# Attention values in two passes: V's high and low parts of one head as one stationary operand

## The chip, the cores and the metric

The kernel runs on one core of a Trainium2 chip. The metric is the device time of one execution in microseconds. TensorE (PE) multiplies matrices into PSUM, VectorE (DVE) and ScalarE (ACT) do the elementwise work, GpSimd (POOL) a little of it, and the DMA queues are driven from SyncE (SP) and GpSimd.

## The reference, cut to what matters

One layer of a mixer (stick-breaking attention, pooling, cross-attention into 256 memory rows, three sigmoid gates), then a mixture of 16 experts with two experts per token. All in float32, 512 tokens, model width 1024, 8 heads of 64 and 4 cross heads of 64. The change touches the last line of each attention:

```python
# stick-breaking attention, per head and block of 128 queries
z = jnp.einsum('bhqd,bhkd->bhqk', qi, k) * scale
log_1m = jnp.where(strict, jax.nn.log_sigmoid(-z), 0.0)
tail = lax.cumsum(log_1m, axis=3, reverse=True) - log_1m
a = jnp.where(strict, jnp.exp(jax.nn.log_sigmoid(z) + tail), 0.0)
return jnp.einsum('bhqk,bhkd->bhqd', a, v)

# cross-attention into memory, per head
p = jax.nn.softmax(s, axis=-1)
o = jnp.einsum('bhqm,bmhd->bqhd', p, v)
```

## The kernel before

Matrix products run on operands of type float32r. To keep float32's precision each operand is split into a high part (a copy, which rounds) and a low part (the difference to the original), and a product is three passes: high x high, high x low, low x high. The helper `three` (lines 464 to 468) issues them. ScalarE makes high parts, VectorE low parts. Weights come in chunks of 128 x 2048 through a ring of three slots (`split_hi`, `split_lo`); a chunk is a stage's unit, and TensorE frees it by `chunk_used`. There is no scheduler: each engine's order is the order of the code, and semaphores tie them.

Stages around the change, by TensorE: projections and cross-attention (`cross_scores`, `cross_transpose`, `cross_out`, rounds r = 0 and 1 of two heads each), then the loop over heads n = 0 to 8 (lines 1269 to 1293). In round n TensorE issues `tails(n)` (20 passes), a projection (24 passes of 512 columns, or 48 of 256) in rounds 0 to 4, 6 and 8 only, then `values(n - 1)` (lines 1233 to 1248) and `scores(n + 2)`. So rounds 5 and 7 have no projection. ScalarE computes the logarithm of head n + 1 (three passes over 128 x 1280, `logarithm`), the exp that gives `attn`, the high parts; VectorE computes `softplus` and the low parts. `attn_hi` exists once, `attn` and `attn_lo` twice.

`values(m)` computes one head's output, transposed, into bank 7 of PSUM: for each of 4 blocks of keys, 512, 384, 256 and 128 query columns wide, the stationary operand is 128 columns of V, which are two heads (64 columns each), and only the 64 rows of the head in question are read out (line 916 for the high part, 1762 for the low). The next `values` waits until both have read the bank (`av_l`, line 1238). `cross_out(r)` does the same with V of the memory: 2 heads x 2 blocks x 3 passes of 512 columns, read out at lines 842 to 847 and 1693 to 1698. `v_hi_part` and `v_lo_part` (lines 820, 1676) make V's two parts, a quarter at a time.

After the heads come four rounds of gates and branches (`rest`), the output product, routing, and the experts.

Of the kernel before, what the change touches and what calls it, by code (L numbers as in the profile page):

```python
# [28 lines left out]
P = 128  # L29
# [66 lines left out]
def build_trunk(nc, x, mem, norm_mix, norm_mem, w_in, w_pool, pool_scale, w_kv_mem, w_up_sb,  # L96
# [80 lines left out]
    v_hi = sb("v_hi", [P, TB, SBW], F32R, "m", 32 * KB)  # L177
    v_lo = sb("v_lo", [P, TB, SBW], F32R, "m", 40 * KB)
# [25 lines left out]
    vm_hi = sb("vm_hi", [P, MB, XW], F32R, "t", 12 * KB)  # L204
    vm_lo = sb("vm_lo", [P, MB, XW], F32R, "t", 14 * KB)
# [74 lines left out]
    with ctx:  # L280
# [52 lines left out]
        xo_ps = sem("xo_ps")  # L333
        xo_h = sem("xo_h")
# [10 lines left out]
        av_ps = sem("av_ps")  # L345
        av_h = sem("av_h")
# [410 lines left out]
        def _(act):  # L757
# [51 lines left out]
            proj_hi(C_VM, vm_hi[:, :, :], bank(1))  # L809
# [32 lines left out]
            def cross_o(r):  # L842
# [18 lines left out]
            qk_hi(2, 2)  # L861
            cross_o(0)
            split_hi(act, K(C_PAIR[2]))
# [28 lines left out]
            cross_o(1)  # L892
            soften(0)
            split_hi(act, K(C_V[1]))
            qk_hi(4, 6)
            for n in range(HEADS + 1):
# [15 lines left out]
                if n >= 1:  # L912
                    m = n - 1
                    rows = slice(DH * (m % 2), DH * (m % 2) + DH)
                    act.wait_ge(av_ps, m + 1)
                    act.activation(sbT_hi[rows, m // 2, :], bank(7)[rows, :], ACT.Copy).then_inc(av_h, 1)
                if n == 3:
                    split_hi(act, K(C_MERGE))
                if n == 5:
                    split_hi(act, K(C_MERGE + 1))  # L920

# [137 lines left out]
        def _(pe):  # L1059
# [86 lines left out]
            def cross_out(r):  # L1146
# [42 lines left out]
            pe.wait_ge(xo_l, 1)  # L1189
# [43 lines left out]
            def values(m):  # L1233
# [3 lines left out]
                if m >= 1:  # L1237
                    pe.wait_ge(av_l, m)
# [28 lines left out]
            pe.wait_ge(xo_l, 2)  # L1267
# [285 lines left out]
        def _(dve):  # L1553
# [99 lines left out]
            dve.wait_ge(proj_h, 3)  # L1653
            less(flat(vm_lo[:, :, :]), bank(1), flat(vm_hi[:, :, :])).then_inc(proj_l, 1)
# [436 lines left out]
```

## Time and profile before

| | us |
|---|---|
| median of 3 runs | 769.59 (769.48 to 770.74) |
| the profiled execution | 769.72 |
| its span, first to last instruction | 767.9 |
| TensorE busy | 713.7 (93%) |
| VectorE busy | 507.8 (66%) |
| ScalarE busy | 407.8 (53%) |
| mean granted clock of TensorE | 0.972 of full speed |

The profile is one execution, taken by the hardware profiler. Times of rows are from the start of the span. TensorE's matmul rows overlap (a row's duration holds the pipeline's fill and drain), so what a pass costs in a stream is the distance between two starts, not its duration. A bracket at the end of a row gives the engine's idle time before it and what released it. The granted clock is 1.00 at 2.4 GHz and 0.50 at 1.2 GHz. Helpers' rows carry the helper's line: L466 to L468 are the three passes of `three`, L443 and L449 are the ring's high and low parts, L1612 is `less`, VectorE's subtraction.

### The profile page before, as it was taken

How to read it: one execution, taken by the hardware profiler on the slowest of the kernel's cores; microseconds unless marked ns; L12 is line 12 of the kernel's file. 1: busy time of each engine (PE TensorE's matmuls, PEld its weight loads, DVE VectorE, ACT ScalarE, POOL GpSimd, SP SyncE). 2: the span in 40 equal slices, each digit the busy share in tenths (PEclk: the TensorE clock that was granted, in tenths of full speed). 3: DMA queues.
4: the chain of work that ended last, by engine and by line, in shares of the span. 5: the costliest groups of instructions: out<-in, count | busy, mean ns of one | idle time of the engine just before them, and what ended most of it. 6: DMA issues, size and time to landing. Idle time of an engine off the chain costs nothing.

```text
span 767.9 us, 9989 instructions
## 1 busy us (share of the span) xinstructions
PE 713.7 (93%) x3587; PEld 598.3 (78%) x3587; DVE 507.8 (66%) x548; ACT 407.8 (53%) x413; POOL 109.5 (14%) x112
## 2 busy tenths in 40 slices
PE   4999998899999999999999999999999999999920
PEld 3898887789888888888888957888888888888810
DVE  5768563456632507062444588999999999999928
ACT  6726555456632214032232427787878787887712
POOL 5000000000000000000000121333334344331120
PEclk9999998999999999999999999999999999999975
DMA  8552321000023322322377169999999999999444
GB/s 275 172 165 55 110 72 38 1 1 28 15 93 113 101 78 90 115 96 96 128 258 299 39 254 362 395 392 373 372 371 371 365 381 364 371 377 374 184 166 189
DMA packets 85169, 155.47 MB, mean 202 GB/s; under 512 B 6229, under 2 KB 37071, under 8 KB 84628
## 3 DMA queue, kind: packets, MB, share of 16 engines
q1 hardware_dynamic: 78452, 137.39, 50.4%
q0 software_dynamic: 6688, 17.69, 6.0%
q8 instruction: 19, 0.31, 0.2%
q14 instruction: 10, 0.08, 0.0%
HBM read 150.64 MB, written 12.58 MB: 213 GB/s over the span
## 4 chain that ended last, share of the span: by engine, by line
PE 88%; DVE 5%; ACT 2%; issue 2%; DMA 2%; POOL 1%; POOLq 0%; DVEq 0%; ACTq 0%
PE ps L466 27%; PE ps L468 26%; PE ps L467 26%; PE ps L1447 2%; PE ps L1227 1%; PE ps L1504 1%; PE ps L1373 1%; PE ps L1473 1%; PE ps L1229 1%; PE ps L1401 1%; DMA y_rows<-ye,y_col 1%; PE ps L1073 1%; DMA y_in<-y_rows 1%; DVE x L2060 1%; DVE x L2067 1%
## 5 line engine op out<-in xcount | busy, mean ns | idle before, releaser
L449 DVE TENSOR_TENSOR ring_lo<-raw_a,ring_hi 128x2048 fp32r<-128x2048 f32 (+2 forms) x58 | 115.5, 1994 | 97.2 <-ACT ring_hi L443 97.2
L449 DVE TENSOR_TENSOR ring_lo<-raw,ring_hi 128x2048 fp32r<-128x2048 f32 x71 | 161.3, 2289 | 12.4 <-ACT ring_hi L443 10.9
L443 ACT ACTIVATE ring_hi<-raw 128x2048 fp32r<-128x2048 f32 x71 | 136.3, 1920 | 19.8 <-PE ps L468 19.8
L466 PE MATMUL ps<-hT_hi,ring_hi 128*128 128x512 f32 x288 | 113.9, 396 | 4.4 <-DVE v_lo L1612 2.2
L443 ACT ACTIVATE ring_hi<-raw_a 128x2048 fp32r<-128x2048 f32 (+2 forms) x58 | 97.4, 1680 | 32.3 <-PE ps L468 32.2
L468 PE MATMUL ps<-hT_hi,ring_lo 128*128 128x512 f32 x288 | 112.8, 392 | 0.0
L467 PE MATMUL ps<-hT_lo,ring_hi 128*128 128x512 f32 x288 | 112.7, 391 | 0.0
L466 PE MATMUL ps<-ring_hi,xT_hi 128*128 128x512 f32 x240 | 94.8, 395 | 1.8 <-DVE xT_lo L1918 1.8
L468 PE MATMUL ps<-ring_hi,xT_lo 128*128 128x512 f32 x240 | 93.8, 391 | 0.0
L467 PE MATMUL ps<-ring_lo,xT_hi 128*128 128x512 f32 x240 | 93.6, 390 | 0.0
L466 PEld LDWEIGHTS ps<-hT_hi,ring_hi 128*128 128x128 f32 x288 | 54.4, 189 | 16.7 <-DVE v_lo L1612 2.4
L468 PEld LDWEIGHTS ps<-hT_hi,ring_lo 128*128 128x128 f32 x288 | 54.5, 189 | 11.6
L467 PEld LDWEIGHTS ps<-hT_lo,ring_hi 128*128 128x128 f32 x288 | 54.5, 189 | 10.9
L723 POOL DMA_INDIRECT y_rows<-ye,y_col x16 | 33.0, 2060 | 177.9 <-DVE ye L2003 174.9
L466 PEld LDWEIGHTS ps<-ring_hi,xT_hi 128*128 128x128 f32 x240 | 45.1, 188 | 11.1 <-DVE xT_lo L1918 2.1
L468 PEld LDWEIGHTS ps<-ring_hi,xT_lo 128*128 128x128 f32 x240 | 45.0, 188 | 9.4
L467 PEld LDWEIGHTS ps<-ring_lo,xT_hi 128*128 128x128 f32 x240 | 45.1, 188 | 9.1
L466 PE MATMUL ps<-ring_hi,aT_hi 128*128 128x512 f32 x120 | 48.1, 401 | 0.0
L468 PE MATMUL ps<-ring_hi,aT_lo 128*128 128x512 f32 x120 | 47.0, 392 | 0.0
L467 PE MATMUL ps<-ring_lo,aT_hi 128*128 128x512 f32 x120 | 46.9, 391 | 0.0
L933 ACT ACTIVATE sig<-ps 128x1024 f32<-128x1024 f32 x8 | 8.2, 1029 | 69.0 <-PE ps L468 69.0
L708 POOL DMA_INDIRECT xe<-h_rows,x_col x15 | 35.0, 2332 | 12.9 <-POOL x_col L705 12.9
(339 smaller groups left out, 1269.2 us busy)
## 6 DMA issues: line engine op xcount, KB each, us to landing
raw<-in_w_down SPq DMA_DIRECT2D x25, 1024.0 KB
raw<-in_w_gate SPq DMA_DIRECT2D x47, 512.0 KB
raw<-in_w_up SPq DMA_DIRECT2D x47, 512.0 KB
raw_a<-in_w_in SPq DMA_DIRECT2D x15, 1024.0 KB
raw_a<-in_w_gate SPq DMA_DIRECT2D x17, 512.0 KB
raw_a<-in_w_up SPq DMA_DIRECT2D x17, 512.0 KB
raw_a<-in_w_down SPq DMA_DIRECT2D x7, 1024.0 KB
raw_a<-in_w_in SPq DMA_DIRECT2D x10, 512.0 KB, 7.9
```

The costliest lines, as they stand in the source:

```text
L443: act.activation(ring_hi[:, c[0] % SPLIT, 0:width], buf[:, 0:width], ACT.Copy).then_inc(hi_ready, 1)
L449: dve.tensor_tensor(ring_lo[:, s, 0:width], buf[:, 0:width], ring_hi[:, s, 0:width].bitcast(F32), ALU.subtract).then_inc(lo_ready, 1)
L466: pe.matmul(out_ap, l_hi, r_hi, start=start, stop=False, skip_group_check=True)
L467: pe.matmul(out_ap, l_hi, r_lo, start=False, stop=False, skip_group_check=True)
L468: return pe.matmul(out_ap, l_lo, r_hi, start=False, stop=stop, skip_group_check=True)
L708: pool.indirect_dma_start(xe[b][:, :], None, h2_rows[:, :], bass.IndirectOffsetOnAxis(x_col[b][:, :].bitcast(U32), 0), bounds_check=S - 1, ...
L723: pool.indirect_dma_start(y_rows[:, :], bass.IndirectOffsetOnAxis(y_col[b][:, :].bitcast(U32), 0), ye[b][:, :], None, bounds_check=2 * S - ...
L933: act.activation(sig[:, i, :, :], gate_pair(i), ACT.Sigmoid).then_inc(g_sig, 1)
L1073: ins = pe.transpose(bank(k)[:, t * P:(t + 1) * P], xn[:, t, k * P:(k + 1) * P], ident[:, :])
L1227: pe.matmul(zz[:, o:o + w], lhs[:, :], soft_hi[:, j:j + w], start=False, stop=False, skip_group_check=True)
L1229: ins = pe.matmul(zz[:, o:o + w], lhs[:, :], soft_lo[:, j:j + w], start=False, stop=jb == TB - 1, skip_group_check=True)
L1447: ins = pe.transpose(bank(2, 2)[:, k * P:(k + 1) * P], xe[b][:, k * P:(k + 1) * P], ident[:, :])
```

## The change

V's two parts go into one array of four blocks of 64 columns per pair of heads, in the order high(even), low(even), low(odd), high(odd). The stationary operand of a head is then its own two blocks side by side, 128 columns again (`stacked`). One pass with the high part of the attention weights and one with the low part give, in PSUM, the high part of V against both in the head's own 64 rows, and the low part of V against both in the other 64 rows. The two halves have to be added: ScalarE copies the other half into the head's rows of an SBUF array (`value_x`, `cross_x`), VectorE adds the PSUM half to it (`value_sum`, `cross_sum`), and the high and low parts are then taken from the SBUF sum (`value_hi`, `value_lo`, `cross_o`), for the values one round later. TensorE waits for the sum (`av_sum`, `xo_sum`) instead of the low part. The product low x low, which three passes leave out, is included. V's parts are written by two instructions of 256 columns instead of one of 512.

```diff
-    v_hi = sb("v_hi", [P, TB, SBW], F32R, "m", 32 * KB)
-    v_lo = sb("v_lo", [P, TB, SBW], F32R, "m", 40 * KB)
+    v_st = sb("v_st", [P, TB, SBW // P, 4, DH], F32R, "m", 32 * KB)
+    sbT_f = sb("sbT_f", [P, 4, S], F32, "m", 72 * KB)
+    xaT_f = sb("xaT_f", [P, 2, S], F32, "m", 92 * KB)
...
+        def stacked(st, h):
+            return st[:, 2 * h:2 * h + 2, :].rearrange("p b d -> p (b d)")
+        def blocks(ap):
+            return ap.rearrange("p (r h d) -> p r h d", h=2, d=DH)
...
@@ ScalarE @@
-                act.activation(v_hi[:, 2 * (i % 2):2 * (i % 2) + 2, 256 * (i // 2):256 * (i // 2) + 256],
-                               bank(b).rearrange("p (t n) -> p t n", t=2), ACT.Copy).then_inc(v_h, 1)
+                for u in range(2):
+                    ins = act.activation(v_st[:, 2 * (i % 2) + u, 2 * (i // 2):2 * (i // 2) + 2, 0:4:3, :],
+                                         blocks(bank(b)[:, u * 256:u * 256 + 256]), ACT.Copy)
+                ins.then_inc(v_h, 1)
...
+            def cross_x(r):
                 act.wait_ge(xo_ps, r + 1)
                 for h in range(2):
-                    rows = slice(DH * h, DH * h + DH)
-                    ins = act.activation(xaT_hi[rows, r, :], bank(6 * r + h)[rows, :], ACT.Copy)
-                ins.then_inc(xo_h, 1)
+                    ins = act.activation(xaT_f[head_rows(h), r, :], bank(6 * r + h)[head_rows(1 - h), :], ACT.Copy)
+                ins.then_inc(xo_x, 1)
+            def value_x(m):
+                act.wait_ge(av_ps, m + 1)
+                act.activation(sbT_f[head_rows(m % 2), m // 2, :], bank(7)[head_rows(1 - m % 2), :],
+                               ACT.Copy).then_inc(av_x, 1)
+            def value_hi(m):
+                rows = head_rows(m % 2)
+                act.wait_ge(av_sum, m + 1)
+                act.activation(sbT_hi[rows, m // 2, :], sbT_f[rows, m // 2, :], ACT.Copy).then_inc(av_h, 1)
...
                 if n >= 1:
-                    m = n - 1
-                    rows = slice(DH * (m % 2), DH * (m % 2) + DH)
-                    act.wait_ge(av_ps, m + 1)
-                    act.activation(sbT_hi[rows, m // 2, :], bank(7)[rows, :], ACT.Copy).then_inc(av_h, 1)
+                    value_x(n - 1)
+                if n >= 2:
+                    value_hi(n - 2)
...
@@ TensorE @@
                     for m in range(MB):
-                        ins = three(pe, bank(6 * r + h), vm_hi[:, m, r * P:(r + 1) * P], vm_lo[:, m, r * P:(r + 1) * P],
-                                    pT_hi[:, 2 * h + m, :], pT_lo[:, 2 * h + m, :], m == 0, m == MB - 1)
+                        pe.matmul(bank(6 * r + h), stacked(vm_st[:, m, r, :, :], h), pT_hi[:, 2 * h + m, :],
+                                  start=m == 0, stop=False, skip_group_check=True)
+                        ins = pe.matmul(bank(6 * r + h), stacked(vm_st[:, m, r, :, :], h), pT_lo[:, 2 * h + m, :],
+                                        start=False, stop=m == MB - 1, skip_group_check=True)
...
                 if m >= 1:
-                    pe.wait_ge(av_l, m)
+                    pe.wait_ge(av_sum, m)
...
-                    ins = three(pe, bank(7)[:, sbk * P:], v_hi[:, sbk, pr * P:(pr + 1) * P],
-                                v_lo[:, sbk, pr * P:(pr + 1) * P], attn_hi[:, o:o + w], attn_lo[m % 2][:, o:o + w],
-                                sbk == 0, sbk == TB - 1)
+                    pe.matmul(bank(7)[:, sbk * P:], stacked(v_st[:, sbk, pr, :, :], m % 2), attn_hi[:, o:o + w],
+                              start=sbk == 0, stop=False, skip_group_check=True)
+                    ins = pe.matmul(bank(7)[:, sbk * P:], stacked(v_st[:, sbk, pr, :, :], m % 2),
+                                    attn_lo[m % 2][:, o:o + w], start=False, stop=sbk == TB - 1, skip_group_check=True)
...
-            pe.wait_ge(xo_l, 2)
+            pe.wait_ge(xo_sum, 2)
             project_qk(4, 6)
...
@@ VectorE @@
+            def value_sum(m):
+                rows = head_rows(m % 2)
+                dve.wait_ge(av_x, m + 1)
+                dve.tensor_tensor(sbT_f[rows, m // 2, :], bank(7)[rows, :], sbT_f[rows, m // 2, :], ALU.add).then_inc(av_sum, 1)
...
+                if n >= 1:
+                    value_sum(n - 1)
                 if n < HEADS:
                     dve.wait_ge(a_exp, n + 1)
-                    if n >= 1:
-                        dve.wait_ge(av_ps, n)
                     dve.tensor_copy(attn_hi[:, :], attn[n % 2][:, :]).then_inc(a_h, 1)
...
-                if n >= 1:
-                    m = n - 1
-                    rows = slice(DH * (m % 2), DH * (m % 2) + DH)
-                    dve.wait_ge(av_h, m + 1)
-                    less(sbT_lo[rows, m // 2, :], bank(7)[rows, :], sbT_hi[rows, m // 2, :]).then_inc(av_l, 1)
+                if n >= 2:
+                    value_lo(n - 2)
```

How the instructions then stand. First TensorE, values of head 1, before (the first passes; the words are output, moving operand, stationary operand, shape and semaphores waited for):

```order
L466 MATMUL ps<-attn_hi,v_hi 128x512 [waits av_l,a_l]
L467 MATMUL ps<-attn_lo_148,v_hi 128x512
L468 MATMUL ps<-attn_hi,v_lo 128x512
L466 MATMUL ps<-attn_hi,v_hi 128x384
L467 MATMUL ps<-attn_lo_148,v_hi 128x384
L468 MATMUL ps<-attn_hi,v_lo 128x384
L466 MATMUL ps<-attn_hi,v_hi 128x256
```

and after, from the same place:

```order
L1282 MATMUL ps<-attn_hi,v_st 128x512 [waits av_sum,a_l]
L1284 MATMUL ps<-attn_lo_148,v_st 128x512
L1282 MATMUL ps<-attn_hi,v_st 128x384
L1284 MATMUL ps<-attn_lo_148,v_st 128x384
L1282 MATMUL ps<-attn_hi,v_st 128x256
L1284 MATMUL ps<-attn_lo_148,v_st 128x256
```

The four passes with V's low part are gone, and the first pass waits for the sum.

VectorE in rounds 5 and 6 of the loop over heads, before. `attn_hi` and `attn_lo` belong to heads 5 and 6, `soft` and `soft_lo` to heads 6 and 7, `sbT_lo` to heads 4 and 5, and `ring_lo` is the low part of a weight chunk:

```order
L1724 SCALAR_TENSOR_TENSOR soft<-ps,log_in 128x1280 [waits tail_ps,z_ln]
L1729 TENSOR_TENSOR soft_lo<-soft,soft_hi 128x1280 [waits soft_h]
L1752 CAST attn_hi<-attn_146 128x1280 [waits av_ps,a_exp]
L1754 TENSOR_TENSOR attn_lo_148<-attn_146,attn_hi 128x1280 [waits a_h]
L1612 TENSOR_TENSOR sbT_lo<-ps,sbT_hi 64x512 [waits av_h]
L449 TENSOR_TENSOR ring_lo<-raw_a,ring_hi 128x2048 [waits hi_ready]
L1724 SCALAR_TENSOR_TENSOR soft<-ps,log_in 128x1280 [waits tail_ps,z_ln]
L1729 TENSOR_TENSOR soft_lo<-soft,soft_hi 128x1280 [waits soft_h]
L1752 CAST attn_hi<-attn_145 128x1280 [waits av_ps,a_exp]
L1754 TENSOR_TENSOR attn_lo_147<-attn_145,attn_hi 128x1280 [waits a_h]
L1612 TENSOR_TENSOR sbT_lo<-ps,sbT_hi 64x512 [waits av_h]
```

and after, where `sbT_f` is the sum of heads 4 and 5, and `sbT_lo` belongs to head 3:

```order
L1780 SCALAR_TENSOR_TENSOR soft<-ps,log_in 128x1280 [waits tail_ps,z_ln]
L1785 TENSOR_TENSOR soft_lo<-soft,soft_hi 128x1280 [waits soft_h]
L1753 TENSOR_TENSOR sbT_f<-ps,sbT_f 64x512 [waits av_x]
L1809 CAST attn_hi<-attn_146 128x1280 [waits a_exp]
L1811 TENSOR_TENSOR attn_lo_148<-attn_146,attn_hi 128x1280 [waits a_h]
L1650 TENSOR_TENSOR sbT_lo<-sbT_f,sbT_hi 64x512 [waits av_h]
L454 TENSOR_TENSOR ring_lo<-raw_a,ring_hi 128x2048 [waits hi_ready]
L1780 SCALAR_TENSOR_TENSOR soft<-ps,log_in 128x1280 [waits tail_ps,z_ln]
L1785 TENSOR_TENSOR soft_lo<-soft,soft_hi 128x1280 [waits soft_h]
L1753 TENSOR_TENSOR sbT_f<-ps,sbT_f 64x512 [waits av_x]
L1809 CAST attn_hi<-attn_145 128x1280 [waits a_exp]
L1811 TENSOR_TENSOR attn_lo_147<-attn_145,attn_hi 128x1280 [waits a_h]
```

The sum stands ahead of `attn_hi` and waits for ScalarE's copy; the low part stands where it stood, for the head before. Between `soft_lo` and the next `soft` there is one instruction of 64 x 512 more.

ScalarE in round 5, before (`log_in` is the logarithm of head 7):

```order
L888 ACTIVATE soft_hi<-soft 128x1280 [waits z_soft]
L916 ACTIVATE sbT_hi<-ps 64x512 [waits av_ps]
L443 ACTIVATE ring_hi<-raw_a 128x2048 [waits chunk_used,raw_full2]
L880 ACTIVATE log_in<-ps 128x1280 [waits z_soft,z_ps]
L882 ACTIVATE log_in<-log_in 128x1280 [waits act_c]
L884 ACTIVATE log_in<-log_in 128x1280 [waits act_c]
```

and after:

```order
L922 ACTIVATE soft_hi<-soft 128x1280 [waits z_soft]
L870 ACTIVATE sbT_f<-ps 64x512 [waits av_ps]
L876 ACTIVATE sbT_hi<-sbT_f 64x512 [waits av_sum]
L448 ACTIVATE ring_hi<-raw_a 128x2048 [waits chunk_used,raw_full2]
L914 ACTIVATE log_in<-ps 128x1280 [waits z_soft,z_ps]
L916 ACTIVATE log_in<-log_in 128x1280 [waits act_c]
L918 ACTIVATE log_in<-log_in 128x1280 [waits act_c]
```

A second copy of 64 x 512 stands ahead of the chunk's high part and of the next logarithm.

## Rows read from the trace of the kernel before

**Rows 1.** The page's 40 slices: TensorE busy, its granted clock, DMA engines, in tenths.
```profile
PE   4999998899999999999999999999999999999920
...
PEclk9999998999999999999999999999999999999975
DMA  8552321000023322322377169999999999999444
```

**Rows 2.** The page's chain of work that ended last, shares by engine.
```profile
PE 88%; DVE 5%; ACT 2%; issue 2%; DMA 2%; POOL 1%; POOLq 0%; DVEq 0%; ACTq 0%
```

**Rows 3.** Waits of TensorE, 112 to 222 us: us in total, times, longest.
```profile
PE ps L1209 <- ACT attn L905: 3.2, 2, 2.9
PE ps L466 <- DVE v_lo L1612: 2.2, 1, 2.2
PE ps L1227 <- DVE soft_lo L1729: 0.6, 1, 0.6
PE ps L466 <- DVE sbT_lo L1612: 0.6, 1, 0.6
```

**Rows 4.** Stretches with a low clock: us, PE busy (instructions), granted clock, DMA, GB/s.
```profile
120.00:128.00 8.00, 7.91 (x36) 0.57 0.00 0
137.00:142.00 5.00, 5.00 (x17) 0.66 0.02 3
428.00:432.00 4.00, 4.00 (x15) 0.57 0.01 4
```

**Rows 5.** Timeline of TensorE, values of one head: start us, us, instruction; then what follows.
```profile
169.05 0.39 PE L466 MATMUL ps<-attn_hi,v_hi 128*128 128x512 f32 x1
...
170.91 0.40 PE L1209 MATMUL ps<-negmask,identb 128*128 128x128 bf16 x4
```

**Rows 6.** Timeline of TensorE, first eight passes of the tails of head 0, and the next.
```profile
114.29 0.39 PE L1227 MATMUL ps<-soft_hi,negtri 128*128 128x512 f32 x1
...
115.52 0.39 PE L1227 MATMUL ps<-soft_hi,negtri 128*128 128x384 f32 x1
```

**Rows 7.** Timeline of TensorE, cross output of round 1 (12 passes), and what follows.
```profile
103.07 0.40 PE L466 MATMUL ps<-pT_hi,vm_hi 128*128 128x512 f32 x1
...
105.82 0.40 PE L1209 MATMUL ps<-negmask,identb 128*128 128x128 bf16 x4
```

**Rows 8.** Timeline of VectorE, attn_lo of an ordinary head.
```profile
159.39 1.49 DVE L1754 TENSOR_TENSOR attn_lo<-attn,attn_hi 128x1280 fp32r<-128x1280 f32 x1
```

**Rows 9.** Timeline of ScalarE, late heads.
```profile
193.00 0.57 ACT L916 ACTIVATE sbT_hi<-ps 64x512 fp32r<-64x512 f32 x1
...
195.28 1.22 ACT L880 ACTIVATE log_in<-ps 128x1280 f32<-128x1280 f32 x1
```

**Rows 10.** Timeline of VectorE, late heads.
```profile
199.61 1.47 DVE L1724 SCALAR_TENSOR_TENSOR soft<-ps,log_in 128x1280 f32<-128x1280 f32 x1
202.42 1.50 DVE L1729 TENSOR_TENSOR soft_lo<-soft,soft_hi 128x1280 fp32r<-128x1280 f32 x1 [1.34 <-ACT soft_hi L888]
205.16 0.83 DVE L1752 CAST attn_hi<-attn 128x1280 fp32r<-128x1280 f32 x1 [1.25 <-PE ps L468]
206.03 1.49 DVE L1754 TENSOR_TENSOR attn_lo<-attn,attn_hi 128x1280 fp32r<-128x1280 f32 x1
207.55 0.69 DVE L1612 TENSOR_TENSOR sbT_lo<-ps,sbT_hi 64x512 fp32r<-64x512 f32 x1
```

**Rows 11.** Timeline of TensorE, late heads (a bracket: idle us before it, releaser).
```profile
191.54 0.38 PE L1209 MATMUL ps<-negmask,identb 128*128 128x128 bf16 x4 [0.33 <-ACT attn L905]
...
204.90 0.45 PE L1227 MATMUL ps<-soft_hi,negtri 128*128 128x512 f32 x1
...
208.39 0.47 PE L466 MATMUL ps<-attn_hi,v_hi 128*128 128x512 f32 x1 [0.55 <-DVE sbT_lo L1612]
```

**Rows 12.** Timeline of VectorE, eight instructions of 256 columns.
```profile
31.71 3.22 DVE L1623 SCALAR_TENSOR_TENSOR memT_lo<-ps,gains,memT_hi 128x256 fp32r<-128x256 f32 x8
```

**Rows 13.** The page's groups: TensorE's loads of stationary operands.
```profile
L466 PEld LDWEIGHTS ps<-hT_hi,ring_hi 128*128 128x128 f32 x288 | 54.4, 189 | 16.7 <-DVE v_lo L1612 2.4
```

More of the change, by code:

```diff
@@ L203, in build_trunk @@
     km_lo = sb("km_lo", [P, 2, MEM], F32R, "t", 10 * KB)
-    vm_hi = sb("vm_hi", [P, MB, XW], F32R, "t", 12 * KB)
-    vm_lo = sb("vm_lo", [P, MB, XW], F32R, "t", 14 * KB)
+    vm_st = sb("vm_st", [P, MB, XW // P, 4, DH], F32R, "t", 12 * KB)
     U0 = 16
@@ L333, in build_trunk @@
         xo_ps = sem("xo_ps")
+        xo_x = sem("xo_x")
+        xo_sum = sem("xo_sum")
         xo_h = sem("xo_h")
@@ L345, in build_trunk @@
         av_ps = sem("av_ps")
+        av_x = sem("av_x")
+        av_sum = sem("av_sum")
         av_h = sem("av_h")
@@ L462, in width_of, with head_rows @@
             return CW
+        def head_rows(h):
+            return slice(DH * h, DH * h + DH)
+        def stacked(st, h):
+            return st[:, 2 * h:2 * h + 2, :].rearrange("p b d -> p (b d)")
+        def blocks(ap):
+            return ap.rearrange("p (r h d) -> p r h d", h=2, d=DH)
         def three(pe, out_ap, l_hi, l_lo, r_hi, r_lo, start, stop):
@@ L808, in _ @@
             proj_hi(C_KM, km_hi[:, :, :], bank(0))
-            proj_hi(C_VM, vm_hi[:, :, :], bank(1))
+            after(act, K(C_VM))
+            for m in range(MB):
+                act.activation(vm_st[:, m, :, 0:4:3, :], blocks(bank(1)[:, m * XW:(m + 1) * XW]),
+                               ACT.Copy).then_inc(proj_h, 1)
             def qk_hi(n, b):
@@ L861, in _ @@
             qk_hi(2, 2)
+            cross_x(0)
+            split_hi(act, K(C_PAIR[2]))
             cross_o(0)
-            split_hi(act, K(C_PAIR[2]))
             act.wait_ge(pool_d, 2)
@@ L891, in _ @@
             v_hi_part(1, 3)
-            cross_o(1)
+            cross_x(1)
             soften(0)
             split_hi(act, K(C_V[1]))
+            cross_o(1)
             qk_hi(4, 6)
@@ L920, in _ @@
                     split_hi(act, K(C_MERGE + 1))
+            value_hi(HEADS - 1)
             act.preload_act_table_set("sigmoid_and_others")
@@ L1188, in _ @@
             project_qk(3, 3)
-            pe.wait_ge(xo_l, 1)
+            pe.wait_ge(xo_sum, 1)
             project_v(0, 0)
@@ L1651, in _ @@
             link(dve.tensor_copy(pool_a[hi_r, 1, U0:], pool_b[hi_r, 1, U0:]))
-            dve.wait_ge(proj_h, 3)
-            less(flat(vm_lo[:, :, :]), bank(1), flat(vm_hi[:, :, :])).then_inc(proj_l, 1)
+            dve.wait_ge(proj_h, 2 + MB)
+            for m in range(MB):
+                ins = less(vm_st[:, m, :, 1:3, :], blocks(bank(1)[:, m * XW:(m + 1) * XW]), vm_st[:, m, :, 0:4:3, :])
+            ins.then_inc(proj_l, 1)
             def cross_max(r):
@@ L1677, in v_lo_part @@
                 dve.wait_ge(v_h, i + 1)
-                part = (slice(2 * (i % 2), 2 * (i % 2) + 2), slice(256 * (i // 2), 256 * (i // 2) + 256))
-                less(v_lo[:, part[0], part[1]], bank(b).rearrange("p (t n) -> p t n", t=2),
-                     v_hi[:, part[0], part[1]]).then_inc(v_l, 1)
+                for u in range(2):
+                    part = v_st[:, 2 * (i % 2) + u, 2 * (i // 2):2 * (i // 2) + 2, :, :]
+                    ins = less(part[:, :, 1:3, :], blocks(bank(b)[:, u * 256:u * 256 + 256]), part[:, :, 0:4:3, :])
+                ins.then_inc(v_l, 1)
             def cross_norm(r):
@@ L1691, in cross_t, with cross_sum, value_lo @@
                 less(flat(pT_lo[:, :, :]), bank(4, 4), flat(pT_hi[:, :, :])).then_inc(xt_l, 1)
+            def cross_sum(r):
+                dve.wait_ge(xo_x, r + 1)
+                for h in range(2):
+                    ins = dve.tensor_tensor(xaT_f[head_rows(h), r, :], bank(6 * r + h)[head_rows(h), :],
+                                            xaT_f[head_rows(h), r, :], ALU.add)
+                ins.then_inc(xo_sum, 1)
             def cross_o(r):
                 dve.wait_ge(xo_h, r + 1)
-                for h in range(2):
-                    rows = slice(DH * h, DH * h + DH)
-                    ins = less(xaT_lo[rows, r, :], bank(6 * r + h)[rows, :], xaT_hi[rows, r, :])
-                ins.then_inc(xo_l, 1)
+                less(xaT_lo[:, r, :], xaT_f[:, r, :], xaT_hi[:, r, :]).then_inc(xo_l, 1)
+            def value_lo(m):
+                rows = head_rows(m % 2)
+                dve.wait_ge(av_h, m + 1)
+                less(sbT_lo[rows, m // 2, :], sbT_f[rows, m // 2, :], sbT_hi[rows, m // 2, :]).then_inc(av_l, 1)
+            def value_sum(m):
+                rows = head_rows(m % 2)
+                dve.wait_ge(av_x, m + 1)
+                dve.tensor_tensor(sbT_f[rows, m // 2, :], bank(7)[rows, :], sbT_f[rows, m // 2, :], ALU.add).then_inc(av_sum, 1)
             cross_norm(0)
@@ L1710, in _ @@
             qk_lo(2, 2)
+            cross_sum(0)
+            cross_max(1)
             cross_o(0)
-            cross_max(1)
             split_lo(dve, K(C_PAIR[2]))
@@ L1732, in _ @@
             v_lo_part(1, 3)
-            cross_o(1)
+            cross_sum(1)
             soft_low(0)
             split_lo(dve, K(C_V[1]))
+            cross_o(1)
             qk_lo(4, 6)
@@ L1766, in _ @@
                     split_lo(dve, K(C_MERGE + 1))
+            value_lo(HEADS - 1)
             with dve.Fori(0, KD // 2) as dp:
```

4 lines of the change are left out of this document (3 added, 1 removed).

## The prediction

> **What bounds the kernel now.** I read the slices of the page first: TensorE is busy nine tenths or more of nearly every slice, at full clock except in a few places [rows 1]. The chain that ended last says the same: 88% of the span is TensorE, 5% VectorE, 2% ScalarE [rows 2]. So an instruction taken off TensorE is worth its issue interval, unless TensorE waits for something a little later anyway. The DMA engines are nine tenths busy in the expert stage [rows 1], but TensorE waits there only once, for VectorE, and the expert weights are requested as buffers come free, so a stage that starts earlier also loads earlier; I take an earlier start to pass through to the end unchanged.
>
> The change lies between 30 and 220 us. I therefore asked for TensorE's waits from 112 to 222 us, where the heads run: 3.2 us for ScalarE's exp (two times, the longest 2.9), 2.2 for the low part of V, 0.6 for soft_lo, 0.6 for sbT_lo [rows 3]. Everything else in that stretch is bound by TensorE. After the two longest waits the granted clock is at its lower level: 0.57 over the 8 us from 120 and 0.66 over the 5 us from 137, which is (1-0.57)x2x8 = 6.9 us and (1-0.66)x2x5 = 3.4 us at 1.2 GHz, in which half the time is lost. It is low again around 428 us, with no wait ahead of it [rows 4].
>
> **What goes.** Values of one head: twelve passes run from 169.05 to 170.91, 1.86 us [rows 5]. The change leaves eight, of the same four widths (512, 384, 256, 128 columns). What eight such passes take, two with each width, is shown by the first row of blocks of the tails: 114.29 to 115.52, 1.23 us [rows 6]. The saving is 1.86 - 1.23 = 0.63 us for each of eight heads, 5.0 us. Cross output: twelve passes of 512 columns from 103.07 to 105.82, 2.75 us [rows 7]; four of the twelve go, 0.92 us in each of two rounds, 1.8 us. Together 6.9 us if nothing else ends later. No pass becomes dearer: all stationary operands were and are 128 columns wide.
>
> The Trainium skill, page "TensorE: Matmul & The Clock Gate", section "Back-to-back issue gap", gives the isolated interval as columns/2.4 + 2.5 ns; by it the 40 passes would be worth 8 x 0.54 + 8 x 0.216 = 6.1 us (an estimate). The same section gives some 131 ns for a 512-column pass in a sustained stream, which would leave about 1 us of the 1.8 for the cross output. The trace has 2.75/12 = 0.229 us there [rows 7], near the first and far from the second, and the trace decides.
>
> **What is added, and what it lies beside.** Per head there is one more ScalarE instruction and one more VectorE instruction on 64 x 512. The old copies of that size take 0.57 us on ScalarE (0.6 where they don't follow another at once) and 0.69 on VectorE [rows 9, 10]. A ScalarE copy from one half of the partitions into the other is not in the trace. I take the old copy's 0.6 us, since neither its size nor its source changes; the bounds are 0.57 below and 1.2 above (crossing costs double). At 1.2 the cross output would reach project_qk(4) 1.2 us later and values(6) would start 0.6 later: 1.8 us of the gain lost.
>
> Heads 0 to 3. TensorE's next values block no longer waits for hi and lo, but only for copy plus sum, 0.6 + 0.69 = 1.3 us behind the block; it needs them a whole head later. But the sum now stands on VectorE ahead of the two attn instructions, which are what the next block really needs. Today attn_lo of an ordinary head ends at 159.39 + 1.49 = 160.9 for a block that starts at 169.05 [rows 5, 8]: 8.2 us of slack, against 0.6 + 0.69 = 1.3 us of delay. The low part (0.69) and ScalarE's hi copy (0.57) fall into idle time behind. All 4 x 0.63 = 2.5 us come through.
>
> Heads 4 to 7, where there is less other TensorE work between blocks. (1) scores(7) starts at 191.54 after a wait of 0.33 us for the exp of head 5 [rows 11]; this exp hangs on scores(6), not on values(4), which lies between. So values(4) becomes shorter and the wait longer, from 0.3 to 0.95 us: 0 of 0.63. (2) tails(6) waits for soft_lo, again behind scores(6): unchanged. (3) On ScalarE, value_x(4) and value_hi(3) now both stand ahead of the split of a weight chunk; the logarithm that began at 195.28 begins 0.5 to 0.6 us later [rows 9]. On VectorE value_sum(4) and value_lo(3), 1.38 us together, replace one sbT_lo of 0.69, so the chunk's low part ends up to 0.7 later, and softplus(7), which started at 199.61 right behind it, starts about 0.6 later. soft_lo(7) would then end at 202.42 + 1.50 + 0.6 = 204.5 [rows 10]. tails(7) started at 204.90 and could now start at 204.3, but gets its operand at 204.55: gain 0.3 instead of 0.6. (4) values(6) started at 208.39, behind sbT_lo (207.55 + 0.69 = 208.24) [rows 10, 11]. Now values(5) ends about 204.4, copy to 205.05, sum to 205.75, the two attn instructions (0.83 and 1.49) to 208.05: values(6) starts near 208.2, gain 0.2. (5) values(6) and values(7) then give 2 x 0.63 = 1.26, since a gate projection of 24 passes (24 x 0.229 = 5.5 us) lies ahead of values(7) and covers the 1.3 + 2.3 us of its operand. Sum for heads 4 to 7: 1.45 us.
>
> Cross output. Today two ScalarE copies and two VectorE subtractions follow it, and TensorE waits for the last; now two copies and two additions of the same size. The wait of project_qk(4) is a chain of the same length from the same point, so 1.8 us come through. The hi and lo splits behind it, now one 128 x 512 each, are off TensorE's path.
>
> V's split. Each part is now two instructions of 128 x 256 instead of one of 128 x 512. Eight VectorE instructions of 256 columns take 3.22 us, 0.40 each [rows 12], so 0.8 against 0.69: 0.1 longer. This counts once, in the wait of 2.2 us before project_qk(5), where v_lo is the last link: 0.1 us lost. Before scores(1) V's part 1 would end level with TensorE's arrival, but a delay there is swallowed by the wait for the cross output behind it.
>
> Sum: 2.5 + 1.45 + 1.8 - 0.1 = 5.7 us. Past the heads ScalarE starts its table load and the third gate chunk about 0.6 us later against TensorE, while TensorE has two gate projections (22 us) before it uses it: nothing. The profiled execution took 769.7 us (767.9 us of span and 1.8 around it), 0.1 above the median of the three runs, so 769.7 - 5.7 = **764.0 us**.
>
> **Rivals.**
> *The clock falls at a new place* (12%). TensorE's idle time between 190 and 209 us grows from 1.5 us in three pieces (0.33, 0.64, 0.55) to some 2.5 in four (0.95, 0.64, 0.3, 0.65). For it: at 428 us the clock is low with no wait at all [rows 4]. Against: pieces of 0.3 to 0.6 cost nothing today, and only waits of 2.2 us or more are followed by the low level in the heads. One such stretch of 3.4 us costs 1.7: 765.7; two 767.4. The reverse is as possible: one of today's stretches may be 3.4 us shorter or absent because work shifted under it, 762.3.
> *The saved passes turn into waits in all heads* (6%). If the ScalarE/VectorE chain bounded the ordinary heads too, only cross output and heads 6 and 7 would count, 1.8 + 1.3: 766.6. For it: heads 4 and 5 do so. Against: no wait at all from 148 to 190 us.
> *Slower* (4%). The sum ahead of attn_hi: value_x + value_sum put 1.3 us between the end of one block and attn_hi, and if TensorE waited for attn_lo at each of seven heads, that would be 7 x 1.3 = 9.0 against 5.7 saved: 769.7 + 3.3 = 773.0. It decides only where attn_lo ends later than 1.3 us before the block; the rows give 8.2 us in an ordinary head, and only head 6 is close; even 1.9 us a head, with the copy at its upper bound, fits into 8.2.
> *No change* (4%): the two-pass form does not go faster, because the stationary operand is loaded anew for each pass (each load 0.19 us [rows 13]) and paces the narrow ones. Against: the tails load anew each time as well [rows 6], 1.23/8 = 0.154 us a pass. It would give 769 to 770.
>
> **Numbers.** The likeliest case, 764.0, has 74%; its own range by the clock's stretches and the copy's bounds is 762.3 to 765.7. The whole range is 762.0 to 767.2. What a measurement of this kernel can tell from no change is 0.2%, 1.5 us. Faster 0.91, same 0.05, slower 0.04.
>
> **What would show it.** Values blocks of eight passes in 1.23 us and cross blocks in 1.83; the wait of scores(7) for attn at about 0.95 us; a new wait of tails(7) for soft_lo of some 0.3; values(6) waiting for attn_lo instead of sbT_lo; the wait for V's low part at 2.3; VectorE's additions at 0.69 and ScalarE's crossing copies at 0.6; the merge stage starting 5.7 us earlier, and the same distance at the end of the experts. It is wrong if crossing copies take over 1.2 us, if TensorE waits in heads 1 to 3, or if the expert stage waits for weights.

## The result and the profile after

The changed kernel takes **765.4 us** (median of 5 runs, 764.06 to 766.66); the kernel before, run on the same chip beside it, 769.75 us (769.48 to 770.74). The ratio is 0.9946, 95% interval 0.9931 to 0.996: 0.5% faster, 4.35 us. The forecast was 764.0 with a range of 762.0 to 767.2, so the time lies inside, 1.4 us above the point. The profiled execution took 765.4 us, its span 763.7, which is 4.2 less than the profiled span before.

The page's busy times and slices (TensorE, granted clock, DMA engines, in tenths):

```profile
PE 707.8 (93%) x3547; PEld 593.1 (78%) x3547; DVE 514.7 (67%) x563; ACT 414.8 (54%) x428; POOL 109.6 (14%) x112
...
PE   4999997999999999999999999999999999999920
...
PEclk9999998999899999999999999999999999999975
DMA  8562320000033231323476269999999999999444
```

TensorE has 40 instructions fewer (3587 before), VectorE and ScalarE have 15 more each. Beside [rows 1], the clock's row has one low slice more: slice 7 (115 to 134 us) is the low place after the long wait for exp, as before, and slice 11 (191 to 210 us) is new. Single slices of TensorE and of the DMA differ by a tenth or so. The chain that ended last is TensorE for 88% of the span, as in [rows 2].

The passes themselves. TensorE's timeline of round 1 of the cross output, with the instruction that follows (start us, us, instruction):

```profile
102.31 0.40 PE L1187 MATMUL ps<-pT_hi,vm_st 128*128 128x512 f32 x1
...
104.16 0.40 PE L1246 MATMUL ps<-negmask,identb 128*128 128x128 bf16 x4
```

and of the values of an ordinary head:

```profile
164.48 0.39 PE L1282 MATMUL ps<-attn_hi,v_st 128*128 128x512 f32 x1
...
165.70 0.40 PE L1246 MATMUL ps<-negmask,identb 128*128 128x128 bf16 x4
```

The distance of the starts counts, not the durations, which overlap. Eight cross passes take 104.16 - 102.31 = 1.85 us (twelve took 2.75 [rows 7]), eight passes of values 165.70 - 164.48 = 1.22 us (twelve: 1.86 [rows 5]).

TensorE's waits from 105 to 218 us (us in total, times, longest):

```profile
PE ps L1246 <- ACT attn L940: 3.9, 2, 2.9
PE ps L481 <- DVE v_st L1650: 2.3, 1, 2.3
PE ps L1282 <- DVE attn_lo L1811: 1.0, 1, 1.0
PE ps L1264 <- DVE soft_lo L1785: 0.6, 1, 0.6
PE ps L481 <- DVE xaT_f L1737: 0.4, 1, 0.4
```

Beside [rows 3], 0.7 us more for exp, and a wait of 1.0 for attn_lo where one of 0.6 for sbT_lo stood (the last row lies ahead of the window of [rows 3]). Where these are, TensorE's timeline tells (in brackets the idle us before the instruction and what ended them):

```profile
107.03 0.50 PE L481 MATMUL ps<-hT_hi,ring_hi 128*128 128x512 f32 x1 [0.37 <-DVE xaT_f L1737]
...
134.88 0.50 PE L481 MATMUL ps<-hT_hi,ring_hi 128*128 128x512 f32 x1 [2.31 <-DVE v_st L1650]
...
140.45 0.39 PE L1282 MATMUL ps<-attn_hi,v_st 128*128 128x512 f32 x1
...
185.69 0.38 PE L1246 MATMUL ps<-negmask,identb 128*128 128x128 bf16 x4 [0.96 <-ACT attn L940]
...
201.25 0.45 PE L1264 MATMUL ps<-soft_hi,negtri 128*128 128x512 f32 x1
...
205.20 0.50 PE L1282 MATMUL ps<-attn_hi,v_st 128*128 128x512 f32 x1 [1.02 <-DVE attn_lo L1811]
...
212.07 0.39 PE L1282 MATMUL ps<-attn_hi,v_st 128*128 128x512 f32 x1
```

The instructions of the kernel before that answer to these and are not in [rows 11], by its timeline:

```profile
108.69 0.50 PE L466 MATMUL ps<-hT_hi,ring_hi 128*128 128x512 f32 x1 [0.36 <-DVE xaT_lo L1612]
...
136.52 0.50 PE L466 MATMUL ps<-hT_hi,ring_hi 128*128 128x512 f32 x1 [2.25 <-DVE v_lo L1612]
...
143.73 0.39 PE L466 MATMUL ps<-attn_hi,v_hi 128*128 128x512 f32 x1
...
215.84 0.39 PE L466 MATMUL ps<-attn_hi,v_hi 128*128 128x512 f32 x1
```

How far ahead of before the changed kernel is, place by place:

| place | ahead, us | step |
|---|---|---|
| project_qk(4) | 1.66 | cross output |
| project_qk(5) | 1.64 | V's split, 0.02 lost |
| values(0) | 3.28 | no pass saved here: 1.64 from the clock |
| scores(7) | 5.85 | values(0) to (3) 2.57; values(4) nothing |
| values(6) | 3.19 | 2.66 given back |
| values(7) | 3.77 | values(6) 0.58 |
| first pass behind values(7) | 4.41 (217.69 before, 213.28 after) | values(7) 0.64 |
| end of the span | 4.2 | 0.2 given back |

The two jumps that belong to no pass are the clock's. Windows of TensorE (us, busy and instructions, granted clock, DMA share, GB/s):

```profile
120.00:128.00 8.00, 8.00 (x42) 0.58 0.00 0
137.00:142.00 5.00, 5.00 (x29) 1.00 0.01 3
188.00:196.00 8.00, 7.36 (x29) 0.57 0.01 3
424.00:428.00 4.00, 4.00 (x14) 0.61 0.01 4
```

The stretch of 0.66 from 137 to 142 us of [rows 4] is absent, which gives the 1.7 us of its 5 x 0.34. From 188 to 196, where the kernel before had full clock, it is 0.57: 7.36 busy us at that clock lose about 0.43 of themselves, 3.2 us. So the profiled 4.2 is no clean measure of the change, and a second one is needed.

**A measure without the clock.** Each run lists its span and its mean granted clock. TensorE sets the pace for most of the span, so I take (1 - clock) x span for the time lost at the lower level and compare kernels by span x clock. It is a measure for differences only: of the 21 us so counted in the kernel before, 14 stand in the last 28 us, where TensorE has no instruction and the profile lists a clock of 0.50 (740 to 768 us; in the changed kernel 736 to 764, also 0.50), and these 14 are the same in every kernel. The clock is given to 0.001 or so, 0.8 us in one run, so I use means over runs; +- is one standard error of the mean.

Before, 29 runs: clock 0.9710, product 746.1 (+-0.1). After, 5 runs: 0.9696 and 740.5 (+-0.2). The difference is **5.5 us** (+-0.2) for a sum of 5.7 forecast; about 1 us of it is then lost because the mean clock was 0.0014 lower. The 29 are the runs of before that stand beside the first four experiments, since those beside the changed kernel have no clock on record; 11 more on another chip, beside the last four experiments, give 746.1 too.

Runs with the same listed clock can be compared directly: at 0.970, 768.86 before (13 runs) and 763.60 after (2 runs), 5.3 us; at 0.972, 767.72 (10) and 762.3 (1), 5.4; at 0.968, 771.0 (1) and 764.65 (2), 6.4, with one run of before only. The clock is also what spreads runs of one kernel: those before at 0.974 lie at 766.25 us of span (2 runs).

### The profile page after: what moved, and what is told of

Its sections match the earlier page's. It is cut to its first block, busy times and chain, and to the rows that moved or that the text cites. A ratio compares the mean times of both kernels' runs of the same rounds, so it can differ in the third digit from the quotient of the medians.

```text
span 763.7 us, 9932 instructions
## 1 busy us (share of the span) xinstructions
PE 707.8 (93%) x3547; PEld 593.1 (78%) x3547; DVE 514.7 (67%) x563; ACT 414.8 (54%) x428; POOL 109.6 (14%) x112
## 4 chain that ended last, share of the span: by engine, by line
PE 88%; DVE 6%; issue 2%; ACT 2%; DMA 2%; POOL 1%; POOLq 0%; DVEq 0%; ACTq 0%
PE ps L481 26%; PE ps L482 25%; PE ps L483 25%; PE ps L1485 2%; PE ps L1264 1%; PE ps L1266 1%; PE ps L1542 1%; PE ps L1411 1%; PE ps L1511 1%; DMA y_rows<-ye,y_col 1%; PE ps L1439 1%; DMA y_in<-y_rows 1%; DVE x L2115 1%; DVE x L2122 1%; PE ps L1284 1%
```

## The experiments

### Cross output alone

The kernel before, with the two-pass form for the cross output only (with its copies and additions, which the cut leaves out); the values keep their three passes.

```diff
-                        ins = three(pe, bank(6 * r + h), vm_hi[:, m, r * P:(r + 1) * P], vm_lo[:, m, r * P:(r + 1) * P],
-                                    pT_hi[:, 2 * h + m, :], pT_lo[:, 2 * h + m, :], m == 0, m == MB - 1)
+                        pe.matmul(bank(6 * r + h), stacked(vm_st[:, m, r, :, :], h), pT_hi[:, 2 * h + m, :], ...)
+                        ins = pe.matmul(bank(6 * r + h), stacked(vm_st[:, m, r, :, :], h), pT_lo[:, 2 * h + m, :], ...)
```

> The kernel before with the cross output alone in two passes (values as before). Theory A (savings add up by pass count where nothing waits): the cross blocks take 1.83 us instead of 2.75, all later waits keep their lengths (2.91 before scores(2), 2.25 before project_qk(5), 0.33, 0.64, 0.55 in the late heads), and the time is 1.8 us below before at an equal share of the low clock. Rival B (the clock decides more than the passes): the time lies anywhere from 1.8 below to 1.8 above before, with the mean granted clock of each run explaining the rest; span x (1 - clock), taken off the span, should then still differ by 1.8 from before.

Measured: 768.63 us (12 runs, 765.98 to 770.59) beside 770.42 of before; ratio 0.9978 (0.9966 to 0.999). Span x clock 744.1, 2.0 below before. TensorE's waits are those of before to 0.1 us. Yet the clock is low from 192 to 196 us, after waits no longer than those in the kernel before. TensorE's timeline at the two waits, and its windows:

```profile
189.14 0.33 PE L1231 MATMUL ps<-negmask,identb 128*128 128x128 bf16 x3 [0.33 <-ACT attn L925]
...
192.28 0.76 PE L1249 MATMUL ps<-soft_hi,negtri 128*128 128x512 f32 x1 [0.63 <-DVE soft_lo L1758]
```

```profile
188.00:192.00 4.00, 3.32 (x23) 1.00 0.00 0
192.00:196.00 4.00, 3.73 (x15) 0.57 0.00 0
```

Nothing near these instructions was changed but their place in time, 2.4 us earlier than in the kernel before.

### Values alone

The changed kernel with the cross output back to three passes. Seen from the kernel before, this is the two-pass form for the values only (its copies and additions are again left out of the cut):

```diff
-                    ins = three(pe, bank(7)[:, sbk * P:], v_hi[:, sbk, pr * P:(pr + 1) * P],
-                                v_lo[:, sbk, pr * P:(pr + 1) * P], attn_hi[:, o:o + w], attn_lo[m % 2][:, o:o + w],
-                                sbk == 0, sbk == TB - 1)
+                    pe.matmul(bank(7)[:, sbk * P:], stacked(v_st[:, sbk, pr, :, :], m % 2), attn_hi[:, o:o + w], ...)
+                    ins = pe.matmul(bank(7)[:, sbk * P:], stacked(v_st[:, sbk, pr, :, :], m % 2), attn_lo[m % 2][:, o:o + w], ...)
```

> The changed kernel with the cross output back to three passes. Theory A: values blocks of 1.23 us; heads 0 to 3 give 2.5 us, head 4 nothing (wait before scores(7) 0.95), heads 6 and 7 give 1.3, V's split costs 0.1: some 3.8 us below before at an equal share of the low clock, and 1.8 above the changed kernel. Rival B: no sum of the two parts is visible because the low-clock stretches move by themselves; then the difference to before is within 1.8 of 3.8 either way, run by run, following the mean granted clock.

Measured: 767.66 us (12 runs, 765.55 to 770.73), ratio 0.997 (0.9957 to 0.9984). Span x clock 742.2 (+-0.2), 3.9 below before; the forecast's steps for values and V's split give 2.5 + 1.45 - 0.1 = 3.85. With the 2.0 (+-0.2) of the cross output this makes 5.9 (+-0.3) for 5.5 (+-0.2) in the whole: the parts add up within their errors. Two of its waits of TensorE are the ones that the changed kernel has more than before:

```profile
PE ps L1237 <- ACT attn L933: 3.9, 2, 2.9
...
PE ps L1273 <- DVE attn_lo L1793: 1.0, 1, 1.0
```

### The short waits filled with passes

The changed kernel, with seven passes of 512 columns around scores(7), whose output nobody reads.

```diff
+                if n == 5:
+                    pe.wait_ge(v_l, 4)
+                    for _ in range(4):
+                        pe.matmul(bank(6), hT_hi[:, 0, 0:P], hT_hi[:, 0, :], start=True, stop=True, skip_group_check=True)
                 if n + 2 < HEADS:
                     scores(n + 2)
+                if n == 5:
+                    for _ in range(3):
+                        pe.matmul(bank(6), hT_hi[:, 0, 0:P], hT_hi[:, 0, :], start=True, stop=True, skip_group_check=True)
```

> The changed kernel with seven more 512-column passes whose result nobody reads: four after values(4), in the wait before scores(7), three after scores(7), in the wait before tails(6). The work is not needed; it keeps TensorE busy. Theory C (the longer wait of 0.96 us with the 0.64 us behind it brings the low clock at 189 us): the stretch of half clock from 189 to 195 us disappears and the time falls by 1.7 to 3.4 us against the changed kernel. Rival D (where the clock falls has nothing to do with this wait): the stretch is still there in some executions and the time is the changed kernel's within 0.3 us, the passes being hidden in the waits.

Measured: 764.34 us (6 runs, 764.02 to 766.87), ratio 0.9935 (0.9919 to 0.9952). Work added on TensorE costs nothing that can be measured, since it stands where TensorE waited (the wait before scores(7) is gone): span x clock 740.7 (+-0.3), the changed kernel's 740.5. In its profile's windows of TensorE the clock from 185 to 200 us is full, but low from 136 to 140, inside the stretch where the changed kernel's was full:

```profile
136.00:140.00 4.00, 4.00 (x12) 0.60 0.00 0
185.00:200.00 15.00, 15.00 (x84) 1.00 0.07 19
```

The mean clock over its runs is 0.9703 beside 0.9696. That is too little to tell apart with so few runs, and its median lies inside the changed kernel's range. So theory C has its stretch gone but not its gain of 1.7 to 3.4 us. One profile each can't tell whether the passes moved the stretch or whether it would have moved by itself.

### The kernel before, with head 4 short

The kernel before, whose head 4 leaves out the product with V's low part (four passes).

```diff
+                    if m == 4:
+                        pe.matmul(bank(7)[:, sbk * P:], v_hi[:, sbk, pr * P:(pr + 1) * P], attn_hi[:, o:o + w], ...)
+                        ins = pe.matmul(bank(7)[:, sbk * P:], v_hi[:, sbk, pr * P:(pr + 1) * P], attn_lo[m % 2][:, o:o + w], ...)
+                        continue
```

> The kernel before with head 4 computed without its four passes of V's low part (this part of the product is left out for head 4). Nothing else changes. The chain from scores(6) through the exp is untouched, so the wait before scores(7) grows from 0.33 to 0.95 us and no time is saved at full clock. Theory C: a stretch of half clock appears behind 190 us and the time rises by 1.7 to 3.4 us above before. Rival D: no such stretch; the time is that of before within 0.3 us.

Measured: median of ten executions 769.64 us (two more, of 1474 and 2552 us, are left out of it), ratio 0.999 (0.9977 to 1.0002), span x clock 746.3 (+-0.1) beside 746.1. Four passes went and the time stayed; they became a wait, as the forecast's step (1) has it. But the clock did not fall behind this longer wait, by TensorE's timeline and window:

```profile
191.56 0.33 PE L1209 MATMUL ps<-negmask,identb 128*128 128x128 bf16 x3 [0.96 <-ACT attn L905]
...
194.70 0.50 PE L1227 MATMUL ps<-soft_hi,negtri 128*128 128x512 f32 x1 [0.64 <-DVE soft_lo L1735]
```

```profile
185.00:200.00 15.00, 13.40 (x85) 1.00 0.00 0
```

After reading the changed profile, my theory was that the wait of 0.33 us, grown to 0.96, brings the low stretch at 188 us. As a rule it falls here: 0.96 and 0.64 us of waiting with full clock behind them, and 0.33 and 0.63 with a low one in the cross-only kernel. That the longer wait makes the low stretch likelier isn't excluded: the two other kernels with a wait of 0.96 at this place have it in their profiles too, values alone (0.82 from 188 to 192 us, 0.50 from 192 to 196) and the next one (0.73 from 185 to 192).

### attn_hi ahead of the sum

The changed kernel; VectorE makes attn_hi of head n first and value_sum(n-1) behind it.

```diff
-                if n >= 1:
-                    value_sum(n - 1)
                 if n < HEADS:
                     dve.wait_ge(a_exp, n + 1)
+                    if n >= 1:
+                        dve.wait_ge(av_ps, n)
                     dve.tensor_copy(attn_hi[:, :], attn[n % 2][:, :]).then_inc(a_h, 1)
+                if n >= 1:
+                    value_sum(n - 1)
```

> The changed kernel with VectorE's order turned back in one point: attn_hi stands ahead of the sum, the sum between attn_hi and attn_lo. Theory A (the wait of 1.02 us before values(6) hangs on the copy's 0.59 us, in which VectorE has nothing to do): copy and attn_hi run side by side, attn_lo of head 6 ends 0.6 us earlier, the wait before values(6) falls to about 0.4, and span x clock is 0.3 to 0.6 us below the changed kernel's. Rival E (the wait is set by soft_lo and the tails ahead of it, not by the sum): no change at equal clock.

Measured: 765.93 us (5 runs), ratio 0.9956 (0.994 to 0.9971); the interval holds the changed kernel's 0.9946. Its effect is seen in the trace; in span x clock, 740.0 (+-0.2), it is 0.5 below, two standard errors of the difference. VectorE's timeline ahead of values(6), first of the changed kernel and then of this one:

```profile
202.07 0.69 DVE L1753 TENSOR_TENSOR sbT_f<-ps,sbT_f 64x512 f32<-64x512 f32 x1 [3.16 <-ACT sbT_f L870]
202.79 0.83 DVE L1809 CAST attn_hi<-attn 128x1280 fp32r<-128x1280 f32 x1
203.66 1.49 DVE L1811 TENSOR_TENSOR attn_lo<-attn,attn_hi 128x1280 fp32r<-128x1280 f32 x1
```

```profile
201.53 0.83 DVE L1809 CAST attn_hi<-attn 128x1280 fp32r<-128x1280 f32 x1 [2.76 <-PE ps L1284]
202.38 0.69 DVE L1753 TENSOR_TENSOR sbT_f<-ps,sbT_f 64x512 f32<-64x512 f32 x1
203.11 1.49 DVE L1814 TENSOR_TENSOR attn_lo<-attn,attn_hi 128x1280 fp32r<-128x1280 f32 x1
```

The cast runs while ScalarE still copies, and the wait of values(6) falls from 1.02 to 0.46 us, as theory A has it.

### The two long waits taken away, in both kernels

ScalarE's q_hi(4) goes behind the logarithm of head 1, and VectorE's low part of V ahead of softplus(2). The same edit was made to the changed kernel and to the kernel before.

```diff
-            qk_hi(4, 6)
...
                     logarithm(n + 1)
+                if n == 0:
+                    qk_hi(4, 6)
...
+                if n == 1:
+                    v_lo_part(2, 6)
                 if n + 1 < HEADS:
                     softplus(n + 1)
-                if n == 1:
-                    v_lo_part(2, 6)
```

> The changed kernel with two instructions in other places: ScalarE makes q_hi of the third pair behind the logarithm of head 1 instead of ahead of it, VectorE makes V's low part 2 ahead of softplus(2) instead of behind it. Theory F (the two waits of 2.9 and 2.3 us come from these orders, and the half clock behind them from the waits): the first wait falls to some 1.4 us, the second to 0, no low clock from 118 to 142 us; 3.8 us less at equal clock, and 1.7 to 5 us more by the clock: 757 to 760 us. Rival G (the low clock comes whatever the waits are): 3.8 us less only, 761.7, with the mean granted clock unchanged at 0.970.

> The same two instructions moved in the kernel before. Theory F: as above, 3.8 us less at equal clock and more by the clock, 761 to 765 us. If the gain of the two passes and the gain of this order are independent, the changed kernel with this order lies 5.3 to 5.7 us below this one at equal clock. Rival H (the waits and the saved passes cover each other): the distance is 4 us or less.

Measured: on the changed kernel 756.8 us (755.12 to 759.95), ratio 0.9847 (0.9823 to 0.987); on the kernel before 762.57 us (761.32 to 765.26), ratio 0.9914 (0.9896 to 0.9932). TensorE's waits, of the first:

```profile
PE ps L1247 <- ACT attn L941: 2.4, 2, 1.4
PE ps L1283 <- DVE attn_lo L1812: 1.0, 1, 1.0
```

The wait for exp fell from 2.9 to 1.4 and the one for V is gone: 3.8 us of waiting. Span x clock fell by 3.6 (to 736.9) and by 3.3 (to 742.8) in the kernel before. The rest of the 8.6 us came from the clock, whose mean rose from 0.9696 to 0.9754. Between the two kernels remain 5.8 us (+-0.2) of span x clock, for 5.5 with the waits: the change is worth the same either way, and rival H (4 us or less) falls.

TensorE's windows behind the remaining wait of 1.4 us: the clock is full in the changed kernel with this edit (first, where a stretch of 0.79 stands later, from 180 to 188 us) and low in the kernel before with it (second), where theory F had forecast none:

```profile
118.00:142.00 24.00, 24.00 (x155) 1.00 0.00 1
180.00:188.00 8.00, 7.36 (x37) 0.79 0.00 1
```

```profile
118.00:124.00 6.00, 5.33 (x26) 0.69 0.00 0
124.00:128.00 4.00, 4.00 (x24) 0.61 0.00 0
```

### All waits filled with work of the kernel itself

The changed kernel with V's low part as in the last experiment, attn_hi ahead of the sum, project_qk(4) in two halves with the tails of head 0 between (q_hi(4) and its low part therefore later, behind the exp of head 0 and behind softplus(1)), and the gate projections cut into pieces of one to six contractions that stand where TensorE waited. The cut shows TensorE's part.

```diff
-            project_qk(4, 6)
+            wh4, wl4 = chunk(K(C_PAIR[2]))
+            proj_part(6, wh4, wl4, 0, P, 0, 4)
...
+                if n == 7:
+                    pe.wait_ge(a_exp, HEADS - 1)
+                    gate_part(1, 0, 3)
...
+                if n == 0:
+                    proj_part(6, wh4, wl4, 0, P, 4, KD).then_inc(q_ps, 1)
...
-                    pe.wait_ge(v_l, 4)
-                    gate_half(0, 0, 0, None)
+                    gate_part(0, 2, KD)
...
-                    pe.wait_ge(a_exp, HEADS - 1)
-                    gate_half(0, 1, 0, None).then_inc(chunk_used, 1)
+                    gate_part(1, 3, KD).then_inc(chunk_used, 1)
...
+                if n == 5:
+                    pe.wait_ge(v_l, 4)
+                    gate_part(0, 0, 1)
                 if n + 2 < HEADS:
                     scores(n + 2)
+                if n == 5:
+                    gate_part(0, 1, 2)
```

> The changed kernel with all of it: attn_hi ahead of the sum; V's low part 2 ahead of softplus(2); project_qk(4) in two halves with tails(0) between them, so that the exp of head 0 is ready for scores(2); and the two gate projections of the late heads cut into pieces (one eighth before scores(7), one eighth behind it, three eighths of the second before tails(7)). No work is added or left out. Theory F: no wait over 0.5 us between 105 and 215 us, full clock throughout, 753 to 757 us. Rival G: about 757 to 759 us, with low clock as often as now.

Measured: **751.6 us** (5 runs, 750.09 to 753.19), ratio 0.9767 (0.9749 to 0.9785): 18 us below the kernel before, 14 below the changed one. TensorE's waits from 100 to 215 us, and its windows:

```profile
PE ps L481 <- DVE xaT_f L1758: 0.4, 1, 0.4
PE ps L1247 <- ACT attn L939: 0.2, 1, 0.2
```

```profile
110.00:215.00 105.00, 104.79 (x618) 1.00 0.12 38
...
412.00:416.00 4.00, 4.00 (x18) 0.74 0.00 0
```

Span x clock is 733.8 (+-0.2), 6.7 below the changed kernel; the waits taken away sum to 7.6. About 7 us more came from the clock, mean 0.9786; in the profile it is full all through the heads. The forecast had put too little on the clock (753 to 757 us).

## Why the prediction was right, and where it was not

- **Values 0.63 us a head, heads 0 to 3:** 1.86 - 1.22 = 0.64 measured, 2.57 us over four heads for 2.5 forecast. TensorE waits for nothing in heads 1 to 3. The rivals of waits in all heads and of no change fall, and so does the slower one: one head of seven has the wait for attn_lo.
- **Cross output 1.8:** each block is 0.90 us shorter, but project_qk(4) starts 1.66 earlier in the one profile, and why 0.14 are missing is open; 2.0 +- 0.2 by the runs with it alone. The chain behind it was of equal length, as forecast (wait 0.37 us, before 0.36).
- **V's split, 0.1 lost:** 0.06; the two instructions take 0.74 us together, not 0.8, and the wait is 2.31 instead of 2.25.
- **Head 4 worth nothing:** shown by the experiment that shortens it alone (wait 0.33 to 0.96, span x clock 746.3 for 746.1).
- **Crossing copies:** 0.59 us on ScalarE, at the value taken, far from the bound of 1.2. Hi from SBUF takes 0.63 for 0.57 forecast; it hides. ScalarE's timeline of an ordinary head:

```profile
153.90 0.59 ACT L870 ACTIVATE sbT_f<-ps 64x512 f32<-64x512 f32 x1 [0.61 <-PE ps L1284]
154.51 0.63 ACT L876 ACTIVATE sbT_hi<-sbT_f 64x512 fp32r<-64x512 f32 x1
```

- **Steps (3) and (4), mis-sized.** The wait of 0.3 us of tails(7) did not appear (no bracket at 201.25), and values(6) waited 1.02 us where some 0.65 were forecast. From the start of values(5) to that of values(6) pass 5.17 us (200.03 to 205.20), set by the chain of copy, sum and the two attn instructions. In the kernel with seven extra passes it is 5.16 (198.80 to 203.96), and there both waits appear, 0.41 at tails(7) and 0.39 at values(6), by TensorE's timeline:

```profile
198.80 0.39 PE L1282 MATMUL ps<-attn_hi,v_st 128*128 128x512 f32 x1
...
200.58 0.50 PE L1264 MATMUL ps<-soft_hi,negtri 128*128 128x512 f32 x1 [0.41 <-DVE soft_lo L1792]
...
203.96 0.50 PE L1282 MATMUL ps<-attn_hi,v_st 128*128 128x512 f32 x1 [0.39 <-DVE attn_lo L1818]
```

So the two share one interval: the forecast's 0.3 + 0.65 = 0.95 stands against 0 + 1.02 here and 0.41 + 0.39 there; the sum was about right and the split wrong. In the changed kernel soft_lo ended at 198.90, 2.35 us ahead of tails(7): the low stretch from 188 us had held TensorE back on its way there.
- **The clock.** The term of the sum that missed is the one I put at zero. Both forms of that rival happened in one profile: the stretch at 137 us went (+1.7) and one came at 188 us (-3.2). That the two partly cancel is luck; with the second alone the profiled execution would have taken 767.1 us (an estimate, 765.4 + 1.7), at the edge of the range. Over runs the changed kernel's mean clock is 0.9696, the execution from which the forecast starts had 0.972, and the difference of 0.0024 is 1.8 us, enough to cover the 1.4 us between 764.0 and 765.4. But that execution lay above its own kernel's mean (0.9710), and what remains for the change, 0.0014 +- 0.0008, isn't clear of noise: that the change itself lowers the clock is not shown. My argument against the rival, that only waits of 2.2 us or more are followed by the low level, is false: 0.63 us was, in the cross-only kernel.
- **Experts:** TensorE's waits behind 215 us are one of 1.9 us for VectorE and one of 0.4 for ScalarE, in the kernel before 1.8 and 0.4. From the pass behind values(7), 4.41 ahead, to the end, 4.2 ahead, 0.2 us was given back; where isn't known.

What stays open is what decides whether the clock falls behind a short wait. The length of the wait alone doesn't (0.96 us without, 0.33 with), and a kernel's runs differ in their mean clock among themselves. Shown is only that without the waits the low stretches of the heads are absent in the profile of the last kernel, and that its mean clock is the highest of all.

## What to carry to other kernels

Price removed passes by the distance between starts in a stream of the same widths, then ask at each wait behind them whether it hangs on the shortened block or on something further back; in the second case the pass is worth nothing, as head 4 here. If runs of one kernel spread with the granted clock, compare span x clock or runs of equal clock, or a gain of 0.5% is read off wrongly: here 5.5 us at equal clock showed as 4.35. In this kernel TensorE's waits cost about twice their length: filling 7.6 us of them with work from elsewhere in the kernel gave 14 us, half of it by the clock. The short wait before scores(7) filled alone, with passes that nobody reads, gave nothing that could be measured.

## What the hardware did that I had not expected

- The granted clock differs between runs of the same program: 0.967 to 0.974 for the cross-only kernel, span 768.8 to 764.2 us.
- Short waits at one place of the code are followed by 1.2 GHz in one kernel and not in another: 0.33 and 0.63 us were (0.57 from 192 to 196 us), 0.96 and 0.64 us were not (1.00 from 185 to 200).
- With no wait of TensorE over 0.4 us, the clock was 1.00 for 105 us on end, while the runs of the kernel before lose some 6 us more to it (span x (1 - clock), 22.3 against 16.0).
- A ScalarE copy of 64 x 512 from PSUM into the other half of the partitions takes 0.59 us; the straight copies of the kernel before took 0.57 [rows 9] to 0.59 (158.46, 171.10 and 184.06 us). One from SBUF to SBUF takes 0.63.
